# Gate projections moved from the projection stages into the attention tiles of a hybrid attention trunk

## The chip, the cores and the metric

The kernel runs on one core of a Trainium2 chip. The metric is the device time of one execution in microseconds (us), taken as the median of several. Engines are named as in the profile: PE (TensorE, matrix products and transposes), PEld (its weight loads), DVE (VectorE), ACT (ScalarE), POOL (GpSimd) and SP (SyncE, which issues the DMAs here). A change within 1% of the time before is about what a measurement of this kernel can't tell from no change.

## What is computed

The reference is a trunk of two residual layers over a sequence of 1024 frames with model width 1024, all in 32-bit floats. Cut to what matters:

```python
# layer 0
u = rms_norm(h, norm_g[0])
cq, ckv, kr, g_a, q_b, k_b, v_b, g_b = split_cols(u @ ab_w_in, AB_SIZES)
o_a = mla_attention(...)          # 8 heads, causal by chunks of 64
o_b = chunk_rel_attention(...)    # 8 heads, band of 9 chunks, relative bias
mixed = concat([o_a * silu(g_a), o_b * silu(g_b)]) @ ab_w_out
# layer 1
u = rms_norm(h, norm_g[1])
q, k, v, g, f = split_cols(u @ fox_w_in, FOX_SIZES)
o = forgetting_attention(...)     # 16 heads, causal, decay bias
mixed = (o * silu(g)) @ fox_w_out
# after each layer
h = h + mixed
h = h + (p[i] @ pe_w[i]) * sigmoid(rms_norm(h, pe_gate_norm[i]) @ pe_gate_w[i])
```

The gates `g_a`, `g_b` (512 columns each) and `g` (1024 columns) are projections of the same normed rows `u` as the queries, keys and values.

## The kernel before, in words

Every matrix product is made in three passes, so that its result is close to 32-bit: each operand is split into a high part (rounded to the matrix engine's `fp32r`) and a low part (what is left), and high x high, high x low and low x high are summed in PSUM. The split is always the same pair: ACT copies the value into `*_hi` (rounding), DVE subtracts that from the value into `*_lo`. `a_hi` and `a_lo` ([128, 8, 1024] each) hold a transposed 1024 x 1024 operand in SBUF for the whole kernel: first the normed rows `u`, later the gated attention outputs.

The program is a chain of stages with a barrier between them; inside a stage each engine runs its own written-out order, coupled by semaphores.

- `stage_ab` (tiles `pa_*`): the norm of `x`, the projections of layer 0 in chunks of weight columns (`Weights`: raw load by SP, `w_hi` by ACT at L173, `w_lo` by DVE at L179, two buffers), each chunk against all frames. Its last four chunks (`G0` and on) are the gates: 16 units of kind `"g"`, each 24 matmuls (L652) with 512 columns moving, then a Silu on ACT and a store to `s_g` in DRAM.
- `stage_attention("mla", ...)` and `stage_attention("chk", ...)`: the two attentions of layer 0, 8 heads each. `stage_attention("fox", ...)`: that of layer 1, 16 heads.
- `stage_oe("m", 0, ...)`: the output projection of layer 0 (units `"o"`), the embedding gate (`"e"`), then the projections of layer 1 (`"qk"`, `"v"` and 16 units `"g"`, L1589, stored to `f_g`). `stage_oe("t", 1, ...)`: output projection and embedding gate of layer 1.

The attention stages are what the change rewrites. A head has 8 tiles of 128 queries; tile `t` has `t + 1` blocks of 128 keys (at most 5 in `chk`). The tiles of all heads are numbered `s`, and every engine walks `s` up, in this order inside an iteration:

- PE: `score(s)` (L1009, with mask products at L1013) into one of two PSUM halves; `turn_p(s - 2)`, the transposes of the probabilities (L1024) in pieces of up to 4 blocks; in even iterations `spread_sums` (two transposes, L1032) and `times_v` (L1047) for the pair of tiles `s - 4`, `s - 3`.
- DVE: `row_max(s)` (L1130, in `chk` L1124); in odd iterations `invert` (L1135); `evacuate(s - 2)`, which makes `pt_lo` (L1144); in odd iterations `take_o` (L1152).
- ACT: in odd iterations `take_far` (L1090); `evacuate(s - 2)`, which makes `pt_hi` (L1080); `exp(s)` (L1069), which waits for `maxed` of tile `s`.

A score may only overwrite its half of PSUM when the exponentials of two tiles ago are done (`wait(pe, maxed if chk else exped, s - 1)`, that is tile `s - 2`). A piece is only turned when the piece two before it has been split (`pt_lo_done`). The PSUM tile `pv` has two buffers. Once per pair of heads, POOL forms gate x inverse sum (`gi`, L1184) and multiplies the output with it (L1188), ACT rounds it into `a_hi` (`give`, L1098) and POOL makes `a_lo` (L1190); for the last pair DVE does POOL's part (L1169 to L1175). SP loads `q`, `k`, `v` of a head and a gate row block of a pair, two buffers each, in the order of its loop over the heads.

Of the kernel before, what the change touches and what calls it, by code (L numbers as in the profile page):

```python
# [15 lines left out]
P = 128  # L16
D = 1024
# [38 lines left out]
def build(nc, x, p, positions, norm_g, ab_w_in, mla_q_norm, mla_w_uq, mla_kv_norm, mla_w_ukv,  # L56
# [12 lines left out]
    s_g = dram("s_g", [FH, 64, S])  # L69
# [5 lines left out]
    f_g = dram("f_g", [FH, 64, S])  # L75
# [31 lines left out]
    a_lo = G.sb("a_lo", [P, KD, S], F32R)  # L107
    ident = G.sb("ident", [P, P])
# [89 lines left out]
    def stage_ab():  # L198
        with ExitStack() as st:
# [10 lines left out]
            table += [cols(KD, w_in, at, 256) for at in (C_GB, C_GB + 256, C_GA, C_GA + 256)]  # L210
            LQ, LK, Q0, K0, MQ, V0, MK, V1, G0 = 0, 1, 2, 4, 6, 7, 8, 9, 10
# [3 lines left out]
            xr = sp.sb("xr", [P, 4, D])  # L215
            staged = xr
            sq = sp.sb("sq", [P, D])
            y = sp.sb("y", [P, 2, 768])
            l_hi = sp.sb("l_hi", [P, 5, S], F32R)
            l_lo = sp.sb("l_lo", [P, 5, S], F32R)  # L220
            g_norm = sp.sb("g_norm", [P, D])
# [4 lines left out]
            spare = sp.sb("spare", [P, 2 * CLIP + 8])  # L226
            t1 = spare[:, 0:512].rearrange("q (a n) -> q a n", a=2)
            rel = spare[0:HEADS, 0:2 * CLIP + 1]
# [36 lines left out]
            units += [("g", c, n) for c in range(G0, NCH) for n in range(4)]  # L265
# [20 lines left out]
            for u, (kind, c, n) in enumerate(units):  # L286
# [12 lines left out]
                if kind not in ("v", "g"):  # L299
                    due = u  # L300
# [4 lines left out]
                if kind == "lk" and n == ST - 1:  # L305
                    steps.append(("tables", 0))

# [4 lines left out]
            for what, n in steps:  # L312
                kind = units[n][0] if what in ("a", "b", "e", "t") else ""
                if what == "e" and kind not in ("v", "g"):
                    norm_at[n] = norms
                    norms += 1
                if what == "e" and kind in ("v", "g", "mk"):
                    outs_at["e", n] = outs
                    if kind != "g":
                        lo_at[outs] = len(lo_at)  # L320
                    stores.append(1)
                    outs += 1
# [42 lines left out]
            pair_g = s_g.rearrange("(c h) q n -> c (h q) n", h=2)  # L365

            with nc.Block() as block:

                @block.sync
                def _(sync):  # L370
# [37 lines left out]
                    sync.dma_start(rel, chk_rel_bias[0]).then_inc(rel_in, 16)  # L408

                    for what, n in steps:  # L410
                        if what == "xt" and n + 4 < ST:
                            sync.wait_ge(turned, jobs_at["xt", n] + 2)
                            load_x(n + 4)
                        if what == "w" and n + 1 < NCH:
# [7 lines left out]
                        if what == "e" and ("e", n) in outs_at:  # L422
# [10 lines left out]
                            else:  # L433
                                m = c - G0
                                pair = (4 + 2 * m if m < 2 else 2 * m - 4) + t // 2
                                store(o, pair_g[pair, :, (t % 2) * HALF:(t % 2 + 1) * HALF], src[:, 0:HALF])
# [19 lines left out]
                def _(act):  # L456
                    act.dma_start(g_norm[:], norm_g[0:1, :].to_broadcast([P, D])).then_inc(gain_in, 16)
# [6 lines left out]
                    def x_norm(t):  # L464
                        act.wait_ge(x_in[t % 4], 16 * (t // 4 + 1))
                        nc.scalar.activation(sq[:], xr[:, t % 4, :], ACT.Square, accum_out=x_ss[:, 0, t:t + 1])\
# [10 lines left out]
                    def evacuate(u):  # L477
# [3 lines left out]
                        if ("e", u) in outs_at:  # L481
                            o = outs_at["e", u]
                            slot_free(o)
                            if kind == "v":
# [3 lines left out]
                                return  # L488
                            if kind == "g":
                                nc.scalar.activation(staged[:, o % 4, 0:HALF], src[:, 0, :], ACT.Silu).then_inc(out_made, 1)  # L490
# [77 lines left out]
                def _(pe):  # L568
# [47 lines left out]
                    def unit(u, part):  # L616
# [28 lines left out]
                        elif kind == "v":  # L645
                            last = tokens(dst[:, 0:256], c, n, a_hi, a_lo, 0, 256)
                        else:
                            w_hi, w_lo = wt.halves(c)
                            block, cols = slice(n // 2 * P, (n // 2 + 1) * P), slice(n % 2 * HALF, (n % 2 + 1) * HALF)
                            for k in range(KD):  # L650
                                for w, a in ((w_hi, a_hi), (w_hi, a_lo), (w_lo, a_hi)):
                                    last = nc.tensor.matmul(dst, w[:, k, block], a[:, k, cols],  # L652
                                                            start=(k == 0 and w is w_hi and a is a_hi),
                                                            stop=(k == KD - 1 and w is w_lo))
# [14 lines left out]
                def _(dve):  # L669
# [8 lines left out]
                    def x_norm(t):  # L678
# [3 lines left out]
                        if t == 0:  # L682
# [3 lines left out]
                                                       in1=g_norm[:], op0=ALU.mult, op1=ALU.mult).then_inc(x_made, 1)  # L686
# [27 lines left out]
                    def evacuate(u):  # L714
                        kind, c, t = units[u]
                        if kind == "g":
                            return
# [156 lines left out]
    def stage_attention(kind, heads, first_pair, q_of, k_of, v_of, g_of, extra_of):  # L874

        mla, chk, fox = (kind == k for k in ("mla", "chk", "fox"))
        NT = ST
        NU = NT // 2
        NPAIR = heads // 2
        TILES = NT * heads  # L880

        def lowest(t):

            return max(0, t - BAND // P + 1) if chk else 0

        def turned(t):

            js = list(range(lowest(t), t + 1))
# [3 lines left out]
        BEFORE = [sum(len(turned(t)) for t in range(n)) for n in range(NT + 1)]  # L892

        def piece(s):

            return BEFORE[NT] * (s // NT) + BEFORE[s % NT]

        def in_units(rows):
            return rows.rearrange("q (u n) -> q u n", u=NU)

        with ExitStack() as st:
            sp = Space(st, kind)
            WIDE = BAND if chk else S
            KROWS = QK if mla else P
            XROWS = QK if mla else 67 if fox else 64
# [863 lines left out]
```

## Time and profile before

| what | us |
|---|---|
| median of 3 runs | 1992.22 |
| lowest and highest run | 1991.86, 2003.53 |
| the profiled execution, own time | 2002.86 |
| span of the profiled execution | 2001.1 |
| PE busy over the span | 1784.1 (89%) |
| DVE, ACT, POOL busy | 954.6, 834.7, 98.4 |
| mean granted clock of PE | 0.955 |

The span runs from the first to the last instruction of the program. A granted clock of 1.0 is 2.4 GHz, 0.5 is 1.2 GHz. In a line of the timeline the columns are start, duration, engine, line, operation, tiles (out<-in), shapes and count, and in brackets the idle time of the engine just before and what ended it. Consecutive instructions of one engine, line and tile are merged into a line.

### The profile page before, as it was taken

The page shows a single profiled execution, that of the slowest core. Times are in us where ns is not written, and L with a number is a line of the kernel's source. Part 1 is how long each engine was busy: PE and PEld are TensorE (multiplying, and loading weights), DVE is VectorE, ACT ScalarE, POOL GpSimd, SP SyncE. Part 2 cuts the span into 40 slices and gives each one's busy share as a digit, 9 for nine tenths or more (in the row PEclk, how much of TensorE's full clock was granted, in tenths as well). Part 3 has the DMA queues.
Part 4 walks back from the last instruction along what each step waited for, and adds up shares of the span by engine and source line. Part 5 has one row for each costly group of instructions (what it writes and reads, how often), then busy time and mean ns, then how long its engine had stood idle before and what let it go on. Part 6 is the DMA issues. An engine that isn't in the chain of part 4 may idle for free. (4 is left out here: it accounts for less than half of the span.)

```text
span 2001.1 us, 31843 instructions
## 1 busy us (share of the span) xinstructions
PE 1784.1 (89%) x12720; PEld 1639.9 (82%) x12720; DVE 954.6 (48%) x1797; ACT 834.7 (42%) x1702; POOL 98.4 (5%) x55
## 2 busy tenths in 40 slices
PE   5999778988996996999989999999968888869998
PEld 5999767867884775999989999998757777769898
DVE  5454556105774665234355444321057777722631
ACT  4433234216773765123153333312157778811410
POOL 0000000000210111000000000000002122100000
PEclk9999989998996998999999999999989999989999
DMA  5064368416423551510123443453174555251211
GB/s 179 22 200 144 116 161 216 126 59 163 122 79 100 149 131 37 185 53 27 48 106 106 127 126 120 125 141 100 47 175 121 140 138 128 64 179 48 64 64 38
DMA packets 178371, 223.94 MB, mean 112 GB/s; under 512 B 12856, under 2 KB 148296, under 8 KB 178224
## 3 DMA queue, kind: packets, MB, share of 16 engines
q1 hardware_dynamic: 177152, 218.43, 38.0%
q0 software_dynamic: 640, 2.62, 0.4%
q8 instruction: 102, 1.67, 0.4%
q10 hardware_dynamic: 432, 0.85, 0.1%
q14 instruction: 45, 0.37, 0.1%
HBM read 150.34 MB, written 77.29 MB: 114 GB/s over the span
## 5 line engine op out<-in xcount | busy, mean ns | idle before, releaser
L1556 PE MATMUL m_acc<-m_w_hi,g_a_hi 128*128 128x256 f32 (+1 forms) x1280 | 371.4, 290 | 19.1 <-DVE m_w_lo L179 14.6
L1556 PE MATMUL m_acc<-m_w_hi,g_a_lo 128*128 128x256 f32 (+1 forms) x1280 | 366.1, 286 | 0.0
L1556 PE MATMUL m_acc<-m_w_lo,g_a_hi 128*128 128x256 f32 (+1 forms) x1280 | 365.7, 286 | 0.0
L1556 PEld LDWEIGHTS m_acc<-m_w_hi,g_a_hi 128*128 128x128 f32 x1280 | 247.0, 193 | 19.5 <-DVE m_w_lo L179 14.8
L1556 PEld LDWEIGHTS m_acc<-m_w_lo,g_a_hi 128*128 128x128 f32 x1280 | 247.3, 193 | 0.0
L1556 PEld LDWEIGHTS m_acc<-m_w_hi,g_a_lo 128*128 128x128 f32 x1280 | 245.8, 192 | 0.0
L611 PE MATMUL pa_acc<-pa_w_hi,g_a_hi 128*128 128x256 f32 (+2 forms) x512 | 156.5, 306 | 15.9 <-DVE pa_w_lo L179 15.9
L1556 PE MATMUL t_acc<-t_w_hi,g_a_hi 128*128 128x256 f32 x512 | 147.2, 287 | 15.8 <-DVE t_w_lo L179 15.8
L611 PE MATMUL pa_acc<-pa_w_hi,g_a_lo 128*128 128x256 f32 (+2 forms) x512 | 151.8, 296 | 0.0
L611 PE MATMUL pa_acc<-pa_w_lo,g_a_hi 128*128 128x256 f32 (+2 forms) x512 | 151.5, 296 | 0.0
L1556 PE MATMUL t_acc<-t_w_hi,g_a_lo 128*128 128x256 f32 x512 | 145.8, 285 | 0.0
L1556 PE MATMUL t_acc<-t_w_lo,g_a_hi 128*128 128x256 f32 x512 | 145.1, 283 | 0.0
L1130 DVE TENSOR_REDUCE fox_neg_max<-fox_scores 128x1 f32<-128x128 f32 (+7 forms) x128 | 96.4, 753 | 54.0 <-PE fox_scores L1009 53.1
L1024 PE MATMUL fox_turn<-g_ident,fox_prob 128*128 128x128 f32 x576 | 89.3, 277 | 32.0 <-DVE fox_pt_lo L1144 31.9
L611 PEld LDWEIGHTS pa_acc<-pa_w_hi,g_a_hi 128*128 128x128 f32 x512 | 99.6, 195 | 16.4 <-issue 16.4
L1144 DVE TENSOR_TENSOR fox_pt_lo<-fox_turn,fox_pt_hi 128x128 fp32r<-128x128 f32 (+2 forms) x192 | 100.2, 550 | 25.2 <-ACT fox_pt_hi L1080 24.4
L1556 PEld LDWEIGHTS t_acc<-t_w_hi,g_a_hi 128*128 128x128 f32 x512 | 98.0, 191 | 16.0 <-DVE t_w_lo L179 16.0
L1069 ACT ACTIVATE fox_prob<-fox_scores,fox_neg_max 128x128 f32<-128x128 f32 (+7 forms) x128 | 94.9, 741 | 35.6 <-DVE fox_neg_max L1130 32.7
L1024 PEld LDWEIGHTS fox_turn<-g_ident,fox_prob 128*128 128x128 f32 x576 | 66.5, 141 | 43.7 <-issue 31.0
L611 PEld LDWEIGHTS pa_acc<-pa_w_lo,g_a_hi 128*128 128x128 f32 x512 | 100.0, 195 | 0.0
L611 PEld LDWEIGHTS pa_acc<-pa_w_hi,g_a_lo 128*128 128x128 f32 x512 | 98.9, 193 | 0.0
L1556 PEld LDWEIGHTS t_acc<-t_w_lo,g_a_hi 128*128 128x128 f32 x512 | 98.7, 193 | 0.0
(284 smaller groups left out, 4154.3 us busy)
## 6 DMA issues: line engine op xcount, KB each, us to landing
m_w_raw<-in_fox_w_in SPq DMA_DIRECT2D x16, 1024.0 KB, 6.0
pa_w_raw<-in_ab_w_in SPq DMA_DIRECT2D x10, 1024.0 KB, 5.7
f_v<-m_pr SPq DMA_DIRECT2D x32, 256.0 KB, 3.1
fox_q<-f_q SPq DMA_DIRECT2D x32, 256.0 KB
fox_k<-f_k SPq DMA_DIRECT2D x32, 256.0 KB
fox_v<-f_v SPq DMA_DIRECT2D x16, 512.0 KB, 3.3
s_mq<-pa_xr SPq DMA_DIRECT2D x32, 192.0 KB, 3.0
s_mk<-pa_xr SPq DMA_DIRECT2D x32, 192.0 KB, 3.0
```

The costliest lines, as they stand in the source:

```text
L611: last = nc.tensor.matmul(dst, a[:, k, t * P:(t + 1) * P], w[:, k, n0:n0 + n], start=(k == 0 and a is m_hi and w is w_hi), stop=(k == kt - ...
L1024: last = nc.tensor.transpose(turn[:, g % 2, m, :], prob[:, s % 3, (j - lo) * P:(j - lo + 1) * P], ident[:])
L1069: nc.scalar.activation(prob[:, s % 3, 0:n], src, ACT.Exp, bias=neg_max[:, s % 4:s % 4 + 1], scale=-1.0 if chk else 1.0, accum_out=total[:, ...
L1130: nc.vector.tensor_reduce(r, scores[:, t % 2, 0:n], AX_X, ALU.max, negate=True).then_inc(maxed, 1)
L1144: nc.vector.tensor_tensor(pt_lo[where], turn[:, g % 2, 0:len(js), :], pt_hi[where].bitcast(F32), ALU.subtract).then_inc(pt_lo_done, 1)
L1556: last = nc.tensor.matmul(dst, a[:, k, t * P:(t + 1) * P], w[:, k0 + k, 0:n], start=(k == 0 and a is m_hi and w is w_hi), stop=(k == kt - ...
```

## The change

1. The gate chunks leave `stage_ab` and `stage_oe` (units `"g"`, `s_g`, `f_g` and their stores and loads are gone).
2. The attention of a layer computes its gates itself. Per head SP loads 256 KB of gate weights (`load_gate`: half of the rows of a block of 128 columns, in pieces of 512 bytes), ACT and DVE split them (`gate_hi`, `gate_lo`), and PE runs one step of 3 matmuls of 512 columns in each tile (`gate_part`), 8 tiles for one unit of 128 x 512 gates, in one PSUM bank `gacc`. In the iteration after the one with the eighth step ACT takes tanh(g/2) (`gate_tanh`) and DVE forms (tanh + 1) x g (`gate_times`); the factor 0.5 that makes this a SiLU is put into `take_far`'s scale.
3. `mla` and `chk` become one stage of 16 heads, `ab`.
4. Outputs gather in a new SBUF tile `og`, shared by all stages: `take_o` adds into it, POOL divides each pair of tiles (`divide`) and applies each finished gate unit (`apply_gate`). The split into `a_hi` and `a_lo` moves to the start of `stage_oe`, 8 steps `"os"`, of which two come before its first unit. Scratch tiles of the other stages now lie in `og`, and the loads of `pr` and of the norm gains wait for the last of these splits. `rel` is loaded after the last x tile.
5. To fit, `pv` has one buffer, `prob` two instead of three, so `row_max` in `chk` now waits for the turning of tile `s - 2`; `far` keeps two units.

The diff, cut to its core:

```diff
+        LATE = 2
+        def gate_unit(s):
+            f = s - LATE
+            return divmod(f, KD) if 0 <= f < KD * NH else None
+        def split_gate(s):
+            c, at = divmod(s, 2 * NT)
+            n = 2 * c + 2 + (at == 11)
+            return n if at in (4, 11) and n < NH else None
...
-            pv = sp.ps("pv", [P, 2, 2, 2 * P])
+            pv = sp.ps("pv", [P, 2, 2 * P])
+            gacc = sp.ps("gacc", [P, HALF])
...
+                    def load_gate(n):
+                        wait(sync, w_lo_done, n)
+                        rows = gates[n // 2].rearrange("(k q) n -> q k n", q=P)[:, 4 * (n % 2):4 * (n % 2) + 4, :]
+                        sync.dma_start(w_raw[:], rows).then_inc(in_w, 16)
...
-                    for hd in range(heads):
+                    for hd in range(NH):
                         load_qk(hd)
-                        if chk:
+                        if kinds[hd] == "chk":
                             load_extra(hd)
+                        if hd == 0:
+                            load_gate(0)
                         load_v(hd)
-                        if hd % 2 == 0:
-                            load_gate(hd // 2)
+                        if hd == 0:
+                            load_gate(1)
+                        elif hd < NH - 1:
+                            load_gate(hd + 1)
...
+                    def gate_part(s):
+                        unit, kt = gate_unit(s)
+                        c, half = divmod(unit, 2)
+                        if kt == 0:
+                            pe.wait_ge(w_lo_done, 2 * c + 2)
+                            wait(pe, g_made, unit)
+                        cols = slice(half * HALF, (half + 1) * HALF)
+                        for w, a in ((w_hi, a_hi), (w_hi, a_lo), (w_lo, a_hi)):
+                            last = nc.tensor.matmul(gacc[:], w[:, c % 2, kt, :], a[:, kt, cols],
...
+                        if kt == KD - 1:
+                            last.then_inc(g_summed, 1)
...
                     def spread_sums(uu):
-                        wait(pe, o_done, uu - 1)
+                        wait(pe, o_done, uu)
...
                         if 0 <= s - 2 < TILES:
                             turn_p(s - 2)
+                        if gate_unit(s) is not None:
+                            gate_part(s)
                         if s >= 4 and s % 2 == 0:
                             spread_sums((s - 4) // 2)
                             times_v((s - 4) // 2)
...
+                    def gate_tanh(unit):
+                        act.wait_ge(g_summed, unit + 1)
+                        wait(act, gated, unit - 2)
+                        nc.scalar.activation(gate[:, unit % 3, :], gacc[:], ACT.Tanh, scale=0.5).then_inc(g_tanh, 1)
...
                         if s < TILES:
                             exp(s)
...
+                        if s < 2:
+                            gate_hi(s)
+                        if split_gate(s) is not None:
+                            gate_hi(split_gate(s))
+                        if s >= KD + LATE and (s - LATE) % KD == 0:
+                            gate_tanh((s - LATE) // KD - 1)
...
+                    def gate_times(unit):
+                        dve.wait_ge(g_tanh, unit + 1)
+                        nc.vector.scalar_tensor_tensor(out=gate[:, unit % 3, :], in0=gate[:, unit % 3, :], scalar=1.0,
+                                                       in1=gacc[:], op0=ALU.add, op1=ALU.mult).then_inc(g_made, 1)
...
                         if s >= 5 and s % 2 == 1:
                             take_o((s - 5) // 2)
...
+                        if s >= KD + LATE and (s - LATE) % KD == 0:
+                            gate_times((s - LATE) // KD - 1)
...
+                    def divide(uu):
+                        at = og[r, hd // 2, cols]
+                        nc.gpsimd.tensor_tensor(at, at, far[r, uu % 2, 1, :], ALU.mult).then_inc(divided, 1)
+                    def apply_gate(unit):
+                        at = og[:, m, half * HALF:(half + 1) * HALF]
+                        nc.gpsimd.tensor_tensor(at, at, gate[:, unit % 3, :], ALU.mult).then_inc(gated, 1)
...
-            steps = [("w", 0)]
+            steps = [("w", 0), ("os", 0), ("os", 1)]
...
                 steps.append(("a", u))
+                if c == O0 and n < ST // 2 - 1:
+                    steps += [("os", 2 * n + 2), ("os", 2 * n + 3)]
...
+                            if c == O0:
+                                pe.wait_ge(o_lo, 2 * n + part + 1)
```

## Rows read from the trace of the kernel before

**Rows 1.** Windows, three attentions: PE, PEld, DVE, ACT, POOL busy, clock, DMA share, GB/s.
```profile
446.20:603.10 156.90, 138.34 (x973) 119.54 (x974) 103.75 (x212) 111.91 (x250) 21.54 (x9) 0.95 0.44 122
...
629.00:795.00 166.00, 148.80 (x877) 119.14 (x877) 102.95 (x291) 106.54 (x260) 21.39 (x9) 0.89 0.42 105
...
1452.60:1766.00 313.40, 257.15 (x1856) 218.84 (x1856) 223.60 (x452) 231.64 (x521) 49.97 (x21) 0.96 0.51 125
```

**Rows 2.** Tile m_acc, the gate products of the second layer.
```profile
L1589 PE MATMUL m_acc<-g_a_hi,m_w_hi x128: 389/397/400, 1358.3 to 1447.6; 128*128 128x512 f32 x128
...
L1589 PE MATMUL m_acc<-g_a_hi,m_w_lo x128: 392/397/400, 1358.8 to 1448.0; 128*128 128x512 f32 x128
```

**Rows 3.** Timeline, end of the projections to the start of attention.
```profile
343.37 0.28 PE L611 MATMUL pa_acc<-pa_w_hi,g_a_lo 128*128 128x256 f32 x1
...
446.22 0.34 SPq L949 DMA_DIRECT2D mla_q<-s_mq  x1
...
455.47 0.47 PE L1009 MATMUL mla_scores<-mla_k,mla_q 96*128 96x128 f32 x1 [13.01 <-DMA mla_kx<-s_mk]
```

**Rows 4.** Timeline of DVE: first to second attention, and the end.
```profile
603.14 1.23 DVE L1130 TENSOR_REDUCE mla_neg_max<-mla_scores 128x1 f32<-128x1024 f32 x1 [0.76 <-PE mla_scores L1009]
...
628.97 0.29 DVE L1124 CUSTOM_DVE_ANT_0 chk_prob<-chk_scores,chk_extra 128x128 f32<-128x128 f32 x1 [10.64 <-PE chk_scores L1009]
...
788.87 0.43 DVE L1152 TENSOR_TENSOR chk_o<-chk_pv,chk_far 64x256 f32<-64x256 f32 x1 [1.87 <-ACT chk_far L1090]
...
793.00 1.23 DVE L1175 TENSOR_TENSOR g_a_lo<-chk_o,g_a_hi 128x1024 fp32r<-128x1024 f32 x1 [1.12 <-ACT g_a_hi L1098]
```

**Rows 5.** Timeline of the first attention, third tile of a head.
```profile
551.11 1.04 PE L1024 MATMUL mla_turn<-g_ident,mla_prob 128*128 128x128 f32 x8
...
552.37 1.29 DVE L1144 TENSOR_TENSOR mla_pt_lo<-mla_turn,mla_pt_hi 128x512 fp32r<-128x512 f32 x2 [0.57 <-ACT mla_pt_hi L1080]
...
553.21 0.30 PE L1024 MATMUL mla_turn<-g_ident,mla_prob 128*128 128x128 f32 x1 [0.42 <-DVE mla_pt_lo L1144]
...
553.35 0.39 PE L1032 MATMUL mla_pv<-g_ident,mla_inverse 128*128 128x128 f32 x2
...
553.91 0.54 DVE L1130 TENSOR_REDUCE mla_neg_max<-mla_scores 128x1 f32<-128x384 f32 x1
...
554.49 0.58 ACT L1069 ACTIVATE mla_prob<-mla_scores,mla_neg_max 128x384 f32<-128x384 f32 x1
```

**Rows 6.** The same place in the second layer.
```profile
1536.59 0.39 PE L1032 MATMUL fox_pv<-g_ident,fox_inverse 128*128 128x128 f32 x2
...
1537.99 0.58 ACT L1069 ACTIVATE fox_prob<-fox_scores,fox_neg_max 128x384 f32<-128x384 f32 x1 [0.92 <-DVE fox_neg_max L1130]
```

**Rows 7.** Timeline of PE: its waits near the end of a head.
```profile
567.14 0.63 PE L1024 MATMUL mla_turn<-g_ident,mla_prob 128*128 128x128 f32 x4 [0.92 <-DVE mla_pt_lo L1144]
...
1549.67 0.52 PE L1024 MATMUL fox_turn<-g_ident,fox_prob 128*128 128x128 f32 x3 [1.02 <-DVE fox_pt_lo L1144]
```

**Rows 8.** Lines 1643 and 1458: 128x512 from PSUM on DVE and ACT, ns.
```profile
L1643 DVE SCALAR_TENSOR_TENSOR m_p_hi<-m_tp,g_gcol,m_pr x32: 745/750/753, 1059.9 to 1260.8; 128x512 fp32r<-128x512 f32 x32
...
L1458 ACT ACTIVATE m_pr<-m_acc x16: 597/597/598, 1364.1 to 1448.5; 128x512 f32<-128x512 f32 x16
L1458 ACT ACT_TABLE_LOAD  x1: 1283/1283/1283, 1358.9 to 1358.9; - x1
```

**Rows 9.** Windows of tile chk_pv: one group at either clock.
```profile
706.59:709.27 2.68, 2.68 (x14) 2.68 (x14) 0.00 (x0) 0.00 (x0) 0.53 1.03 219
711.90:713.44 1.54, 1.54 (x14) 1.54 (x14) 0.43 (x1) 0.00 (x0) 1.00 0.30 98
```

**Rows 10.** Windows of PE: after idle stretches of 3 us.
```profile
113.00:116.40 3.40, 3.39 (x29) 1.00 0.54 214
...
1051.20:1054.60 3.40, 3.36 (x16) 0.50 0.00 0
```

**Rows 11.** DMA issues in the first attention, us to landing.
```profile
mla_v<-s_v SPq DMA_DIRECT2D x8, 512.0 KB, 3.7
```

More of the change, by code:

```diff
@@ L298, in stage_ab @@
                 steps.append(("e", u))
[L299 removed]
+                if kind not in ("v",):
                     due = u
@@ L644, in unit @@
                                 last = tokens(acc[:, banks[u][i], :], c, n, l_hi[:, 3:5], l_lo[:, 3:5], HALF * i, HALF)
-                        elif kind == "v":
+                        else:
                             last = tokens(dst[:, 0:256], c, n, a_hi, a_lo, 0, 256)
[L647 to L654, printed above, removed]
                         last.then_inc(summed, 1)
@@ L871, in stage_ab, with stage_attention, chk, lowest @@
             sp.end()
-    def stage_attention(kind, heads, first_pair, q_of, k_of, v_of, g_of, extra_of):
-        mla, chk, fox = (kind == k for k in ("mla", "chk", "fox"))
+    def stage_attention(tag, heads, gates):
         NT = ST
         NU = NT // 2
[L879 to L888, printed above, removed]
+        NH = len(heads)
+        TILES = NT * NH
+        LATE = 2
+        kinds = [head[0] for head in heads]
+        def chk(s):
+            return kinds[s // NT] == "chk"
+        def lowest(s):
+            return max(0, s % NT - BAND // P + 1) if chk(s) else 0
+        def turned(s):
+            js = list(range(lowest(s), s % NT + 1))
             cut = (len(js) + 1) // 2 if len(js) > 4 else 4
             return [js[n:n + cut] for n in range(0, len(js), cut)]
[L892 to L899, printed above, removed]
+        PIECE = [0]
+        for s in range(TILES):
+            PIECE.append(PIECE[-1] + len(turned(s)))
+        QKDMA = {"mla": 4, "chk": 5, "fox": 7}
+        def qk_loaded(hd):
+            return 16 * sum(QKDMA[kind] for kind in kinds[hd % 2:hd + 1:2])
+        def x_loaded(hd):
+            return 16 * sum(kind == "chk" for kind in kinds[hd % 2:hd + 1:2])
+        def gate_unit(s):
[5 more added lines that the diff above has]
+            return n if at in (4, 11) and n < NH else None
         with ExitStack() as st:
[L902 to L905, printed above, removed]
+            sp = Space(st, tag)
             q = sp.sb("q", [P, 2, S], F32R)
@@ new lines, in apply_gate @@
+                    def apply_gate(unit):
+                        m, half = divmod(unit, 2)
+                        pool.wait_ge(divided, NU * (2 * m + 1) + 2 * half + 2)
+                        pool.wait_ge(g_made, unit + 1)
+                        at = og[:, m, half * HALF:(half + 1) * HALF]
+                        nc.gpsimd.tensor_tensor(at, at, gate[:, unit % 3, :], ALU.mult).then_inc(gated, 1)
+                    for uu in range(NU * NH):
+                        divide(uu)
+                        if uu % (2 * NU) in (NU + 1, 2 * NU - 1):
+                            apply_gate(uu // (2 * NU) * 2 + (uu % (2 * NU) == 2 * NU - 1))
@@ L1581, in unit @@
                                 return
[L1582 removed]
+                        else:
                             last = tokens(dst[:, 0:table[c][1]], c, n, a_hi, a_lo, 0, KD, table[c][1])
[L1584 to L1591 removed]
                         last.then_inc(summed, 1)
```

336 lines of the change are left out of this document (149 added, 187 removed).

## The prediction

> **What bounds the kernel now.** I read the page for the stages, then windows over the attentions, then the timeline of one head on all engines, because the change moves work between stages with different limits. In the three attention stages PE is busy for 138 of 157, 149 of 166 and 257 of 313 us, starts and ends included, against 104, 103 and 224 for DVE [rows 1]. So PE has no large idle time there to give away: the reader should see that the attention tiles are already nearly full of matrix work, cut up by short waits. The granted clock is lowest, 0.89, in the second attention, though no PE idle stretch inside its heads reaches 1 us.
>
> The gate products are pure PE work as well. In the second layer 384 matmuls of 512 columns start between 1358.3 and 1448.0 us, 89.7 / 383 = 0.234 us each [rows 2]. The question is therefore not what they cost but what idle time they fill, and what new waits they bring.
>
> **What goes.** The gate units of the projections. First layer: the last other matmul starts at 343.4 and the attention's first load at 446.2 [rows 3]. What remains is the drain of the last k/v tile (its scaling, transposes and four stores, about 9 us by the same drain elsewhere in the stage, instead of the 3.7 us after the last gate): 93 us gone. Second layer: 90 us. The join of the two attentions: row_max of the last mla tile starts at 603.1, that of the first chk tile at 629.0, 25.8 us; in a running stage the next tile would come 2.7 us later, so 23 go, and with chk's slow first head (21.5 against 18.2 us, from the starts of its row_max) 26. The ends: from the last take_o, 788.9, to the end of a_lo, 794.2 [rows 4], 5.4 us become about 2.3 of POOL (multiplications of 256 and 512 columns; those of 1024 take 2.4), 3 us in each layer, 6 in all. Together 93 + 90 + 26 + 6 = 215 us.
>
> **What comes: the products.** Each of 256 tiles gets 3 matmuls, 3 x 0.234 = 0.70 us, so 179 us. That is nearly the 183 removed.
>
> **What comes: a wait at each unit.** There is one PSUM bank for the gates. In iteration s = 8k + 2 (the third tile of a head) PE must begin the next unit, and `g_made` lets it only when tanh and `gate_times` of the old unit are done. Both stand in their queues behind work that hangs on this same iteration's score: tanh behind `exp(s)`, that behind `row_max(s)`. Walk it in the first attention [rows 5], where the eight transposes of tile 7 are followed by the next score at 551.90. With the new step of tile 9 in between, score(10) ends at 551.90 + 0.70 + 0.72 = 553.3, the one transpose by 553.45. DVE is held by pt_lo of tile 7 (to 553.66) and `take_o`, so row_max(10) stays at 553.91 to 554.45 and the exponential at 554.49, with the read of its sum to 555.15. Then tanh, 0.60, and `gate_times`, 0.75 [rows 8], with 0.1 for the hand-over: PE goes on at 556.65. It idles for 3.2 us, and the times_v that began at 553.35 begins at 557.35, 4.0 us later, two gate steps included. Behind PE's wait stand times_v and the next score, and everything else waits for those; ACT and DVE are not full (71% and 66% in [rows 1]), but they have nothing to do then. In the second layer the exponential starts at 1537.99 and times_v at 1536.59 [rows 6]: 1537.99 + 0.67 + 0.60 + 0.10 + 0.75 + 0.05 + 0.70 = 1540.86, 4.3 us later, of which 3.6 are idle. chk by the same steps gives 4.05.
>
> The other six steps of a head cost 6 x 0.70 = 4.2, less what they hide. Near the head's end PE waits 0.92 us for pt_lo in mla and 1.02 in fox [rows 7]; a step in front hides 0.70 of it; fox has 0.5 more in smaller waits. Per head: mla 4.0 + 4.2 - 0.7 = 7.5, chk 4.05 + 4.2 - 0.55 = 7.7, fox 4.3 + 4.2 - 1.2 = 7.3. A stage has 15 such waits; first heads have none. Sum: 7 x 7.5 + 8 x 7.7 + 15 x 7.3 = 224 us.
>
> First heads: 4.2 - 1 for the steps, and a wait of their own. SP loads the second weight half only when DVE has split the first, after the first tile; ACT stands in front of exp(2) until it lands. Load 3.7 to 4.4, two splits of 0.6 and 0.7, against a PE that would be there after 2.5: 5 us. With the steps 8 per stage, 16 us.
>
> **Weight halves later on.** The odd halves are issued right behind the v load of a new head, which waits for times_v of the stalled iteration, and ACT asks for them one iteration later. The v load lands after 3.7 us [rows 11]; a half behind it, smaller but in short pieces, perhaps after 4. ACT is held for 1.5 to 2.3 us in front of exp of the fifth tile. PE needs that exponential 1 to 2 iterations later, so between 0 and 2.1 us show, 0.7 taken, 14 times: 10 us (0 to 30).
>
> **The rest.** `os`: one ACT copy and one DVE subtraction in front of the first output unit, of which 1.6 us show, twice: 3 us; the later ones lie beside units of 5.7 us on PE. `divide` and `apply_gate` lie on POOL, which is idle for over 90% of the time; take_o of the same pair is ready 2 us before the single `pv` is wanted again. The third prob buffer: row_max in chk waits for one to five more transposes, which end before DVE is free in the stalled tile and otherwise are needed only 4 us later: 0, at most 0.5 per tile (32 us).
>
> **The clock.** A times_v group of 14 took 2.68 us at a granted clock of 0.53 and 1.54 at 1.00 [rows 9]: a fall costs 1.1. After two idle stretches of PE of 3.0 us the clock was 1.00 in one case and 0.50 in the other [rows 10]. The new waits are as long, so half of 30 are taken to bring a fall: 15 x 1.1 = 17 us; the bounds are 0 and 34. The Trainium skill, "TensorE: Matmul & The Clock Gate" (What's actually happening), says that the slow clock is the default and only activity lifts it. Taken strictly it speaks against this change, since it would let every one of these idle waits end at the slow clock; the sum would be 17 us more.
>
> **Sum.** 224 + 16 + 10 + 3 + 17 = 270, less 215: +55 us. On the profiled execution's 2002.9 that is 2058; that execution lies 10.6 us above the median of the runs, so the forecast is 2047.
>
> **Rivals.**
> A. The wait for `g_made` doesn't show (faster). With more work on PE, ACT and DVE may run ahead, so that the unit is ready when PE arrives. For: both have a third of their time free. Against: exp(s) can't run ahead of score(s), which PE does just before. Price: the idle 7 x 3.2 + 8 x 3.3 + 15 x 3.6 = 103 and the 17 of the clock go: 1927. It decides once the waits average less than 3.4 x (1 - 55 / 120) = 1.8 us.
> B. Part of it: hand-overs and waits overlap more than I walked, and about half of the wait shows: 2047 - 60 = 1987.
> C. Every wait brings the clock down: 2064. The rule above is this case.
> D. The weight halves land late, and 3 us show each time: 14 x 2.3 = 32 more, 2079.
> E. Tanh and exp don't share ACT's function table. A table load takes 1.28 us in this trace; two more in each of 30 waits is 77, so 2124. The Trainium skill, "ScalarE: Activation LUTs" (Table sets: the hidden batching unit), lists tanh in the set of exp, and by it no load comes.
> F. The change does not move the work (the steps stay at the stage's end): excluded by the order in the diff.
>
> **Chances.** Forecast 0.50, A 0.13, B 0.11, C 0.14, D 0.09, E 0.03. More than 1% faster is below 1972, more than 1% slower above 2012, the least that a measurement of this kernel can tell from no change: faster 0.14, same 0.11, slower 0.75. The range leaves out A and E: 1985 to 2090.
>
> **What would show it.** In the profile after: no gate products before 450 us; PE idle stretches of about 3 us before the gate matmuls in the third tile of every head, ended by DVE's `gate_times`, 15 in each attention stage; heads of about 26 us in the first layer and 25 in the second instead of 19 and 18; ACT waiting for `w_raw` in the fourth tile of even heads; one table load per attention stage. It would be wrong if the gate matmuls started without a wait in the third tile, if heads were shorter than 24 us, or if the attentions together grew by less than 215 us.

## The result, and the profile after

The changed kernel takes 2103.09 us, median of 4 runs (2101.98 to 2105.20); the kernel before takes 1995.45 us (1991.86 to 2003.53, 4 runs). The ratio is 1.0526, with a 95% interval of 1.0502 to 1.0550. It is slower, as forecast, but by 107.6 us in place of 55, and the time lies outside the range of 1985 to 2090. The profiled execution took 2101.98 us, with a span of 2100.1 us against 2001.1 before.

To see which term is off, cut both traces at the first and the last row maximum of each attention. The timeline of VectorE in the kernel before, for the cuts that [rows 4] doesn't have:

```profile
778.89 0.82 DVE L1124 CUSTOM_DVE_ANT_0 chk_prob<-chk_scores,chk_extra 128x640 f32<-128x640 f32 x1 [0.92 <-PE chk_scores L1009]
...
1463.45 0.29 DVE L1130 TENSOR_REDUCE fox_neg_max<-fox_scores 128x1 f32<-128x128 f32 x1 [8.57 <-PE fox_scores L1009]
...
1745.39 1.23 DVE L1130 TENSOR_REDUCE fox_neg_max<-fox_scores 128x1 f32<-128x1024 f32 x1 [0.25 <-PE fox_scores L1009]
```

and the same places in the changed kernel:

```profile
363.65 0.29 DVE L1158 TENSOR_REDUCE ab_neg_max<-ab_scores 128x1 f32<-128x128 f32 x1 [14.77 <-PE ab_scores L1016]
...
820.79 0.82 DVE L1154 CUSTOM_DVE_ANT_0 ab_prob<-ab_scores,ab_extra 128x640 f32<-128x640 f32 x1 [2.18 <-PE ab_turn L1030]
...
1415.60 0.29 DVE L1158 TENSOR_REDUCE fox_neg_max<-fox_scores 128x1 f32<-128x128 f32 x1 [8.46 <-PE fox_scores L1016]
...
1844.13 1.23 DVE L1158 TENSOR_REDUCE fox_neg_max<-fox_scores 128x1 f32<-128x1024 f32 x1 [1.29 <-PE fox_scores L1016]
```

The first row maximum comes 92.8 us earlier (363.7; 456.5 before, read like [rows 4]). The first layer's attentions take 457.1 us in place of 322.4. The stretch between the layers takes 594.8 in place of 684.6, the second attention 428.5 in place of 281.9, and the rest is 0.3 us longer. What went is as forecast, to within a microsecond or two. What came is the whole miss, and it lies inside the heads. Windows over the two attentions of the changed kernel, and over two neighbouring heads of the first (columns as in [rows 1]):

```profile
363.70:829.50 465.80, 407.02 (x2284) 326.44 (x2283) 225.12 (x543) 236.97 (x543) 65.13 (x78) 0.90 0.31 78
641.00:673.00 32.00, 28.34 (x135) 21.86 (x135) 13.24 (x38) 14.49 (x36) 5.59 (x7) 0.79 0.33 78
673.00:699.40 26.40, 22.88 (x135) 17.59 (x135) 13.25 (x39) 14.45 (x36) 2.79 (x5) 1.00 0.38 92
1415.60:1854.00 438.40, 368.29 (x2233) 308.19 (x2233) 237.75 (x479) 243.03 (x543) 65.32 (x78) 0.91 0.34 82
```

The two heads have the same 135 matmul groups. They lie in the part with `chk` heads. One took 26.4 us at a granted clock of 1.00, which is what the prediction walked out for such a head (19 + 7.7). The other took 32.0 us at 0.79. The clock was forecast to fall in half of the waits.

The waits themselves are on the page, in the costliest groups of instructions. The last column is TensorE's idle time before the gate products:

```profile
L1042 PE MATMUL ab_gacc<-g_a_hi,ab_w_hi 128*128 128x512 f32 x128 | 66.8, 522 | 48.7 <-DVE ab_gate L1192 44.7
L1042 PE MATMUL fox_gacc<-g_a_hi,fox_w_hi 128*128 128x512 f32 x128 | 63.7, 498 | 51.3 <-DVE fox_gate L1192 46.8
```

`gate_times` ended 15 of them in each stage, for 44.7 and 46.8 us. One wait in the timeline, the answer to [rows 6]:

```profile
1500.59 0.58 ACT L1090 ACTIVATE fox_prob<-fox_scores,fox_neg_max 128x384 f32<-128x384 f32 x1 [0.66 <-DVE fox_neg_max L1158]
1501.07 0.19 ACT L1090 ACTIVATION_READ_ACCUMULATOR fox_prob<-fox_scores,fox_neg_max 128x1 f32 x1
1501.16 0.59 ACT L1117 ACTIVATE fox_gate<-fox_gacc 128x512 f32<-128x512 f32 x1
1501.78 0.69 DVE L1192 SCALAR_TENSOR_TENSOR fox_gate<-fox_gate,fox_gacc 128x512 f32<-128x512 f32 x1 [1.03 <-ACT fox_gate L1117]
...
1502.62 0.76 PE L1042 MATMUL fox_gacc<-g_a_hi,fox_w_hi 128*128 128x512 f32 x1 [3.00 <-DVE fox_gate L1192]
```

It is the chain of the forecast, link by link: exponential, its sum, tanh, multiplication, TensorE. But the product that follows takes 0.76 us instead of 0.47. Windows of TensorE from there on, over the next products and `times_v` (PE busy, clock, DMA share, GB/s):

```profile
1502.60:1506.00 3.40, 3.38 (x13) 0.50 0.02 5
1506.00:1509.40 3.40, 3.40 (x18) 0.66 0.10 20
648.90:662.50 13.60, 13.60 (x46) 0.52 0.20 60
```

The third row follows a wait of 3.0 us in the first attention: the engine was busy for all of 13.6 us, at half speed for nearly all of it. In the trace's records of the granted clock 26 low stretches begin inside the heads, 12 in the first layer and 14 in the second, of 3.4 to 13.7 us and 150.2 us in all; TensorE was busy for 141.5 us of them. 24 began during one of the 30 waits for `gate_times` or within 1.5 us of its end. The other two, both in the second layer, began 2.0 us after a shorter wait, for ScalarE's exponential. One of these, with the window behind it:

```profile
1567.84 0.50 PE L1016 MATMUL fox_scores<-fox_k,fox_q 128*128 128x512 f32 x1 [1.36 <-ACT fox_prob L1090]
...
1569.80:1573.20 3.40, 3.40 (x13) 0.50 0.02 5
```

The kernel before has 3 low stretches of 3.4 us there, all in its second attention, where no single wait of TensorE inside the heads reached 0.9 us.

### The profile page after: what moved, and what is told of

Same layout as the page of the kernel before. It is cut to its first block and busy times, and to the rows that moved or that the text cites. A ratio compares the mean times of both kernels' runs of the same rounds, so it can differ in the third digit from the quotient of the medians.

```text
span 2100.1 us, 32171 instructions
## 1 busy us (share of the span) xinstructions
PE 1826.9 (87%) x12720; PEld 1665.2 (79%) x12720; DVE 979.9 (47%) x1860; ACT 841.1 (40%) x1724; POOL 139.9 (7%) x176
## 5 line engine op out<-in xcount | busy, mean ns | idle before, releaser
L1101 ACT ACTIVATE ab_pt_hi<-ab_turn 128x384 fp32r<-128x384 f32 (+2 forms) x192 | 82.5, 463 | 77.8 <-PE ab_turn L1030 76.8
L1172 DVE TENSOR_TENSOR fox_pt_lo<-fox_turn,fox_pt_hi 128x128 fp32r<-128x128 f32 (+2 forms) x192 | 99.9, 548 | 22.8 <-ACT fox_pt_hi L1101 21.7
L1222 POOL TENSOR_TENSOR g_og<-g_og,fox_far 64x256 f32<-64x256 f32 x64 | 46.7, 730 | 956.4 <-DVE g_og L1180 956.4
L1597 PEld LDWEIGHTS t_acc<-t_w_hi,g_a_hi 128*128 128x128 f32 x512 | 98.5, 192 | 13.7 <-issue 13.7
L1042 PE MATMUL ab_gacc<-g_a_hi,ab_w_hi 128*128 128x512 f32 x128 | 66.8, 522 | 48.7 <-DVE ab_gate L1192 44.7
L1042 PE MATMUL fox_gacc<-g_a_hi,fox_w_hi 128*128 128x512 f32 x128 | 63.7, 498 | 51.3 <-DVE fox_gate L1192 46.8
L1101 ACT ACTIVATE fox_pt_hi<-fox_turn 128x128 fp32r<-128x128 f32 (+2 forms) x192 | 87.9, 489 | 35.7 <-PE fox_turn L1030 33.8
```

What stands on the lines that cost most here:

```text
L1042: last = nc.tensor.matmul(gacc[:], w[:, c % 2, kt, :], a[:, kt, cols], start=(kt == 0 and w is w_hi and a is a_hi), stop=(kt == KD - 1 and ...
L1101: nc.scalar.activation(pt_hi[u % 2][:, at:at + len(js), (s % 2) * P:(s % 2 + 1) * P], turn[:, g % 2, 0:len(js), :], ACT.Copy).then_inc(pt_ ...
L1172: nc.vector.tensor_tensor(pt_lo[u % 2][where], turn[:, g % 2, 0:len(js), :], pt_hi[u % 2][where].bitcast(F32), ALU.subtract).then_inc(pt_l ...
L1222: nc.gpsimd.tensor_tensor(at, at, far[r, uu % 2, 1, :], ALU.mult).then_inc(divided, 1)
L1597: last = nc.tensor.matmul(dst, a[:, k, t * P:(t + 1) * P], w[:, k0 + k, 0:n], start=(k == 0 and a is m_hi and w is w_hi), stop=(k == kt - ...
```

## The experiments

Ten kernels were run, each beside runs of the kernel before on the same chip (medians 1996.03 and, for the last two, 1999.09 us).

**1. The clock's share.** TensorE is kept busy during the wait with work that nobody reads; the wait stays.

```
                             pe.wait_ge(w_lo_done, 2 * c + 2)
+                            if unit and s - 2 < TILES:
+                                pe.wait_ge(pt_lo_done, PIECE[s - 2])
+                                for r in range(23):
+                                    nc.tensor.transpose(turn[:, (PIECE[s - 2] + 1) % 2, r % 4, :], ident[:], ident[:])
                             wait(pe, g_made, unit)
```

Expected:

> Edit: while PE would wait for the unit it makes 23 transposes that nobody reads (into the free half of the transpose PSUM), after the previous half has been split; order, waits and all other work stay. Theory 1 (24 of 30 waits bring the granted clock down to 0.5 for 3.4 us, and the dense work after the wait pays 1.5 us for each): the clock stays at 1.00 in the attention heads, 25 to 40 us faster than the changed kernel, 2063 to 2078. Theory 2 (a fall costs little, because what follows is limited by ACT and DVE anyway): within 8 us of 2103, or slower by the transposes that overrun the wait.

Measured: 2041.36 us, ratio 1.0219 (1.0182 to 1.0256), 62 us less than the changed kernel. Windows from the first to the last row maximum of each attention:

```profile
363.40:783.70 420.30, 405.06 (x2585) 330.01 (x2585) 220.34 (x530) 232.75 (x534) 62.53 (x75) 0.99 0.34 87
1377.40:1782.80 405.40, 376.57 (x2522) 316.85 (x2522) 231.62 (x467) 237.83 (x533) 62.63 (x75) 0.98 0.37 89
```

Two low stretches are left in the heads, both begun within 2.2 us of the end of a wait of 1.3 to 1.4 us for the exponential, and the attentions take 420.3 and 405.4 us in place of 457.1 and 428.5: 60 us, for 24 fewer stretches, or 2.5 us each. Nothing but TensorE's idle time was changed, so this 60 is the clock. Theory 1 had the mechanism and, with 25 to 40 us, too small a size. The 60 fits the low stretches themselves: TensorE did 141.5 us of work in them at half speed, so at most half of that, 71 us (an estimate), could be lost.

The same with 10 transposes, so that part of each wait stays idle:

> As the run that kept TensorE busy with 23 unread transposes during each wait (2041 us), but with only 10, so that something near 2 us of each wait stays idle; nothing waits longer for it. Theory 1 (the cost of the clock falls with the idle time that is left in a wait, and is nearly gone at 2 us): 2041 to 2055 us. Theory 2 (any idle stretch at this place brings the fall with it): 2080 to 2105 us. In the trace: 2 to 6 falls in the heads by theory 1, over 20 by theory 2.

Measured: 2048.96 us, ratio 1.0269 (1.0248 to 1.0289). The page has no large wait here, so this is the answer for the tile:

```profile
  DVE fox_gate L1196: 21.7, 15
```

TensorE still idled 21.7 us in 15 waits (1.4 us each; 22.2 us in the first layer), and the clock fell 5 times in the heads, 3 times after one of these waits and twice after one for the exponential. This is theory 1 in time and in falls, though less idle time was left than the 2 us that it speaks of. At this size of wait most of the loss is gone already.

**2. The order.** First the odd half of the next weights, on which ScalarE had stood for 0.6 to 2.1 us in each odd head after the first (all its waits for gate weights, those of the first heads included, were 23 with 30.0 us in the changed kernel):

```
-            n = 2 * c + 2 + (at == 11)
-            return n if at in (4, 11) and n < NH else None
+            n = 2 * c + 2 + (at == 13)
+            return n if at in (4, 13) and n < NH else None
```

> Edit: the odd half of the gate weights is split in the sixth tile of its head (s % 16 = 13) instead of the fourth (11); nothing else. Theory 1 (the late weight half costs far more than the 0.7 us per head that I took, about 3, because ACT and DVE both stand still in front of the exponential and row_max that PE needs next): 14 odd heads get 2.5 to 3.5 us shorter, the kernel 35 to 50 us faster than the changed kernel, near 2060, and odd heads of the second layer fall from 29.0 to about 26. Theory 2 (odd heads are longer for another reason, such as the two-tile rhythm of the buffers, or the price only moves to the sixth tile): within 10 us of 2103.

Measured: 2088.40 us, ratio 1.0454 (1.0391 to 1.0517). That is 15 us less than the changed kernel by the medians, between the two theories, but with two runs that lie 9 us apart and an interval that overlaps that of the changed kernel (from 1.0502). ScalarE's waits for gate weights fell from 30.0 to 6.7 us, and the waits for `gate_times` stayed (44.8 and 46.8 us). The clock still fell 28 times in the heads, and was low for 174 us there in place of 150, so the 15 us are net of more low clock. The stall is a side matter.

Then the first step of a unit behind `times_v` in TensorE's order, so that independent work stands ahead of the wait:

```
-                        if gate_unit(s) is not None:
+                        first = gate_unit(s) is not None and gate_unit(s)[1] == 0
+                        if gate_unit(s) is not None and not first:
                             gate_part(s)
...
                             times_v((s - 4) // 2)
+                        if first:
+                            gate_part(s)
```

> Edit: only the first gate step of each unit goes behind times_v in PE's order; tanh and gate_times stay where they are. Theory 1 (PE idles 3.1 to 3.5 us per unit because it asks for the unit before ACT and DVE can have finished it): times_v of 2.3 us fills the wait, so 0.8 to 1.2 us of idle is left, 30 x 2.3 = 69 us less, and the falls of the clock go as well, up to 37 more: 2000 to 2035. Theory 2 (the wait is only moved: ACT and DVE need PE's next score, which now comes no earlier): 2085 to 2105.

Measured: 1969.57 us, ratio 0.9859 (0.9826 to 0.9892): 133.5 us less than the changed kernel. The tile's answer in the second layer:

```profile
  DVE fox_w_lo L1190: 4.6, 1
  DVE fox_gate L1195: 3.8, 15
```

46.8 us of waits became 3.8 (44.7 became 7.8 in the first layer), 80 us less in all, and no low stretch begins any more between the first and the last row maximum of either attention. The time lies below theory 1's 2000 to 2035: the waits shrank by more than it expected, and it priced the clock at 37 at most. 80 and the clock's 62 would be 142; the other 8 were not traced.

The other end of the same wait, with TensorE's order as in the changed kernel: tanh and its multiplication come first in their iteration.

```
                     for s in range(TILES + 4):
+                        if s >= KD + LATE and (s - LATE) % KD == 0:
+                            gate_tanh((s - LATE) // KD - 1)
...
-                        if s >= KD + LATE and (s - LATE) % KD == 0:
-                            gate_tanh((s - LATE) // KD - 1)
```

and the same for `gate_times` on VectorE.

> The order of TensorE stays as in the changed kernel; only the tanh of a finished unit and its multiplication come first in their iteration of ScalarE and VectorE, ahead of the row sum, the row maximum and the halves that stand ahead of them now. Theory 1 (time goes where TensorE waits, and each wait costs itself and a fall of the clock): the 30 waits shrink from 3.1 to 3.5 us to about 2.3, which gives 30 x 0.9 = 27 us, and of the 62 us of the clock a part in proportion or more, together 45 to 75 us: 2030 to 2060 us. Theory 2 (the clock answers to any recurring wait of this size, whether 3.3 or 2.3 us long): only the waits shrink, 2070 to 2085 us. Theory 3 (the wait is not what costs; ScalarE and VectorE hold the heads): no gain, 2100 us.

Measured: 1992.69 us (8 runs), ratio 0.9980 (0.9963 to 0.9997): 110 us less, beyond all three. The timeline and the tile's answer show why:

```profile
1498.92 0.42 PE L1016 MATMUL fox_scores<-fox_kx,fox_qx 67*128 67x384 f32 x1
...
1499.18 0.61 ACT L1117 ACTIVATE fox_gate<-fox_gacc 128x512 f32<-128x512 f32 x1
...
1500.17 0.69 DVE L1192 SCALAR_TENSOR_TENSOR fox_gate<-fox_gate,fox_gacc 128x512 f32<-128x512 f32 x1
...
1500.97 0.19 PEld L1042 LDWEIGHTS fox_gacc<-g_a_hi,fox_w_hi 128*128 128x128 f32 x1 [1.64 <-issue]
1501.00 0.47 PE L1042 MATMUL fox_gacc<-g_a_hi,fox_w_hi 128*128 128x512 f32 x1 [1.48 <-DVE fox_gate L1192]
```

```profile
  DVE fox_gate L1192: 20.0, 15
  DVE fox_w_lo L1187: 4.4, 1
```

Tanh no longer stands behind an exponential that hangs on this iteration's row maximum. The waits shrank to 20.0 and 17.6 us (from 46.8 and 44.7), which is 54 us, not the 27 expected; one low stretch is left in the heads, and that one followed a wait of 1.3 us for the exponential. 54 and the clock's 60 are the 110 within 4 us. Theory 1 had the mechanism and half of the size.

Both orders together, the second step on the way to the best version:

> Edit: as before, and tanh goes in front of ACT's copies and exponential of that iteration, gate_times in front of DVE's row_max. Theory 1: PE arrives after gate_times has ended, no PE wait over 1 us is left at a unit's start, a further 20 to 30 us less than with the PE order alone: 1975 to 2010. Theory 2 (what is taken from PE's wait comes back, since row_max of the third tile now starts 0.75 us later and everything hangs on it): no faster than with the PE order alone.

Measured: 1949.51 us, ratio 0.9759 (0.9719 to 0.9799). No gate product of a later unit waits any more. That is 20 us less than with TensorE's order alone, as theory 1 had it; its range of 1975 to 2010 started from a time too high for that order. Against the run that keeps TensorE busy and keeps the waits it is 92 us less, and the waits of the changed kernel were 91.5 us.

**3. What the products cost.** On that version's order, 23 of each unit's 24 products are left out:

```
-                        for w, a in ((w_hi, a_hi), (w_hi, a_lo), (w_lo, a_hi)):
-                            last = nc.tensor.matmul(gacc[:], w[:, c % 2, kt, :], a[:, kt, cols],
-                                                    start=(kt == 0 and w is w_hi and a is a_hi),
-                                                    stop=(kt == KD - 1 and w is w_lo))
                         if kt == KD - 1:
-                            last.then_inc(g_summed, 1)
+                            nc.tensor.matmul(gacc[:], w_hi[:, c % 2, kt, :], a_hi[:, kt, cols],
+                                             start=True, stop=True).then_inc(g_summed, 1)
```

> Leaves out 23 of the 24 gate products of each of the 32 units (so the gates are wrong); loads, halves, tanh and multiplication stay. On the order of the run with both changes of order, 1949.5 us. Theory 1 (after the waits are gone TensorE bounds the heads, so each product costs its full 0.234 us): 32 x 23 x 0.234 = 172 us less, 1778 us, with heads of 18.1 to 19.3 us as before the change. Theory 2 (ScalarE and VectorE bound the heads by then, with the halves, the tanh and the multiplications that came to them, 2.6 us of ScalarE and 2.1 us of VectorE per head): heads of about 21 us, 32 x 3 = 96 us less, 1850 us.

Measured: 1931.08 us, ratio 0.9678 (0.9659 to 0.9697). 172 us of matmuls went, and 18 us of time. Neither theory had that. The timeline of that kernel, where the odd half of the weights is split:

```profile
534.16 0.63 ACT L1123 ACTIVATE ab_w_hi<-ab_w_raw 128x512 fp32r<-128x512 f32 x1 [1.80 <-DMA ab_w_raw<-in_ab_w_in]
...
534.83 0.69 DVE L1187 TENSOR_TENSOR ab_w_lo<-ab_w_raw,ab_w_hi 128x512 fp32r<-128x512 f32 x1 [2.56 <-ACT ab_w_hi L1123]
535.43 0.82 DVE L1158 TENSOR_REDUCE ab_neg_max<-ab_scores 128x1 f32<-128x640 f32 x1
...
536.28 0.79 ACT L1090 ACTIVATE ab_prob<-ab_scores,ab_neg_max 128x640 f32<-128x640 f32 x1 [1.11 <-DVE ab_neg_max L1158]
...
537.22 0.79 PE L1016 MATMUL ab_scores<-ab_k,ab_q 96*128 96x512 f32 x1 [2.40 <-ACT ab_prob L1090]
```

ScalarE stands for the transfer, VectorE stands for ScalarE with the row maximum behind it, and 2.40 us of TensorE go idle where the products had been. The clock falls with it (0.89 and 0.91 over the two attentions, as in the changed kernel): 16 low stretches begin in the heads, 119.5 us in all, with TensorE busy for 110 us of them, so up to 55 us (an estimate) are the clock. With the products in place this wait was mostly hidden under them. So it was repeated with the split at position 13:

> The run with one gate product of 24 once more (the gates are wrong again), now with the odd half of the weights split at position 13, when it has landed. In the run before, ScalarE stood 1.8 us for that half, TensorE then idled 2.6 us behind it and the clock fell in nearly every second head. Theory 1 (that wait is what kept the 172 us of products from showing): heads near the 18 to 19 us of the kernel before in place of 20 to 24.5, about 30 x 3.5 = 105 us less than the 1931 us, 1800 to 1850 us. Theory 2 (ScalarE and VectorE hold the heads by their own work): 1900 to 1930 us.

Measured: 1866.55 us, ratio 0.9339 (0.9310 to 0.9368), 80 us less than the next kernel, which differs from it only in having all products. That is 0.11 us for each of 736 products that last 0.234. The clock takes a part of the gain: without the products 7 low stretches begin in the heads, with TensorE busy for 22 us of them, and none with the products, so up to 11 us (an estimate) belong to it. Even so about half of the products' time doesn't show. That it lies beside waits which TensorE has in any case is the reading here; no run separates the products by their place. The time lies between the theories: the heads are at 20.7 and 20.2 us, above the 18 to 19 of the kernel before.

**4. The best version.** Both orders, and the odd half at position 13:

> The run with both changes of order, with the odd half of the next unit's weights split at the iteration after next (position 13 of 16 instead of 11), when its transfer has landed. Theory 1 (ScalarE's wait of 1.3 to 2.1 us for the transfer still delays the heads): 30 x 0.5 to 1.0 = 15 to 30 us less, 1920 to 1935 us. Theory 2 (with TensorE as the bound, a wait of ScalarE is inside its slack): 1945 to 1955 us, no change that can be measured.

Measured: 1946.88 us, ratio 0.9750 (0.9733 to 0.9766): within theory 2, and by the time nothing that can be told from the version without it. The traces say more. From the first to the last row maximum the two attentions take 728.7 us in place of 738.7, mostly because the odd heads of the second layer fell from 23.5 to 22.2 us; in this execution the first row maximum came 4.9 us later (367.2 in place of 362.3), before any code in which the two versions differ, and that hid half of it. Then with the first unit's weights ahead of everything:

```
+                    load_gate(0)
                     for hd in range(NH):
                         load_qk(hd)
...
+                    gate_hi(0)
+                    gate_hi(1)
                     for s in range(TILES + 4):
```

and `gate_lo(0)`, `gate_lo(1)` ahead of VectorE's loop.

> The best run so far (both changes of order, odd half split at position 13, 1947 us) with the first unit's two weight halves loaded ahead of the first head's queries and keys, and split before the first row maximum, while the stage waits for its first transfer. Theory 1 (the waits of 4.3 and 4.7 us for them are on the path that sets the end): 9 us less, 1936 to 1940 us. Theory 2 (the transfers of queries and keys start later by as much): no change, 1944 to 1950 us.

Measured: 1942.03 us, ratio 0.9712 (0.9690 to 0.9733), 5 us less by the medians, and 8 by the ratios, since the two versions ran on different chips. The first heads went from 24.5 to 19.2 and from 23.6 to 18.8 us, but the first score now waits longer for its keys:

```profile
365.94 0.48 PE L1015 MATMUL ab_scores<-ab_k,ab_q 96*128 96x128 f32 x1 [17.29 <-DMA ab_kx<-s_mk]
```

That is 2 us more than the 15.21 us of the run before it. The 10 us of the heads are theory 1, and the later transfers of theory 2 take 2 of them back. This version is 2.9% faster than the kernel before, and 7.7% faster than the change as it was made, with the same products.

## Why the prediction was right in sign and wrong in size

By its own steps, in us against the kernel before. Column A is the sum of the prediction without its 17 for the clock; B is the changed kernel; C is the run that keeps TensorE busy.

| stretch | A, forecast | B, changed | C, kept busy |
|---|---|---|---|
| until the first row maximum | -93 | -92.8 | -93.1 |
| first to last row maximum, layer 1 | +101 | +134.7 | +97.9 |
| from there to the second layer's first | -91.5 | -89.8 | -90.9 |
| first to last row maximum, layer 2 | +122.5 | +146.6 | +123.5 |
| rest | -1.5 | +0.3 | -0.1 |
| sum | +38 | +99.0 | +37.3 |

A for layer 1 is 7 x 7.5 + 8 x 7.7 + 8 for the first head, less 26 for the join, and 5 for the halves. For layer 2 it is 15 x 7.3 + 8 + 5. The middle is -90 - 3 + 1.5.

- **What goes** (215): right.
- **The products and the wait at each unit** (224): right in the first layer, some 12 us too high in the second. The 30 waits were forecast at 3.2 to 3.6 us of idle and came at 3.0 (44.7 / 15) and 3.1 (46.8 / 15) on average. With the clock out of the way the mean head is 26.6 us in the first layer (19 and 19, plus 7.5 and 7.7) and 25.7 in the second (18 + 7.3). The products were taken at their full 0.70 us per step less 0.55 to 1.2 per head. In the order of the changed kernel the sum over a head bears that out in the first layer; in the better order about half of their time is hidden, which the prediction had not asked about.
- **First heads** (16): right. They grew by 8.0 and 8.9 us, forecast 8 each; the waits for the second half were 4.0 and 4.5 us, forecast 5.
- **Weight halves later on** (10): too low, and balanced by luck, so the mean heads above hide two errors. In the run that keeps TensorE busy most odd heads of the second layer take 26.6 us and the even ones 24.4, against 18.1 and 17.9 before: an odd head pays 2.0 us for its half, forecast 0.7, and an even one grew by 6.5, forecast 7.3. The first four odd heads of the first layer pay 0.6 each, the rest about nothing. The halves come to some 16 us (an estimate), 6 more than forecast, while products and wait in 15 heads of the second layer come to 12 less. Rival D, at 32 more in all, is out: the two stretches C of the attentions sum to 221 us, forecast 224.
- **The third `prob` buffer** (0): no loss can be seen. In the kept-busy run the inner `chk` heads take 26.2 to 26.4 us, forecast 26.7 without it. VectorE does wait there for the turning (114.9 us over 54 waits in the changed kernel); a version with three buffers was not run.
- **Tables**: ScalarE loads a table twice in the two attention stages, at the exponential and never at tanh (before, twice in three stages); rival E is out.
- **The clock** (17, bounds 0 and 34): this is the step that failed. The prediction priced a fall at 1.1 us, as a single `times_v` group at low clock, and let half of the 30 waits bring one. Measured: 26 low stretches in place of 15, 24 of them at the 30 waits, and 2.5 us for each, 60 to 62 in all. Even its upper bound, one fall at 1.1 for each wait, was little more than half of that. The price was wrong because a low stretch doesn't end with the group: 150.2 us over 26 stretches is 5.8 us each, and TensorE was busy for 141.5 us of it. The clock's own bounds were taken from one group [rows 9] and from two earlier idle stretches [rows 10], and neither row shows how long the low clock lasts.

In the profiled executions the miss is 2102 - 2058 = 44 us, which is 62 - 17 = 45. Against the median the miss is 56 us. The other 12 come from the correction: the prediction took 10.6 us off because the profiled execution of the kernel before was a long one, but that of the changed kernel lies 1.1 us below its median.

Rival C (every wait brings the clock down, 2064) was nearer in the count, 30 for 24, and had the same wrong price. Rivals A and B fell with the 30 waits. The point from which A was said to decide, waits below 1.8 us, has a near test: with tanh first they averaged 1.25 us, and the kernel came out level with the one before.

As for the rule of the Trainium skill that the prediction weighed ("TensorE: Matmul & The Clock Gate", What's actually happening: the slow clock is the default, and only activity lifts it): the runs bear out that activity decides. Work that nobody reads, put into the waits, kept the clock at 0.98 to 0.99 and gave 62 us. Taken as strictly as the prediction took it, that every idle wait ends at the slow clock, it goes too far: 6 of the 30 waits of 2.8 to 3.3 us brought no fall, and neither did 27 of the 30 of 1.3 to 1.6 us.

## What to carry to other kernels

Independent work that is put between the steps of a tuned loop may fit in its throughput and still lose by one wait in its order. Before the change is judged, ask what the engine's next instruction is when the buffer isn't free, and put the waiting step behind work that can go on. Two reorderings, of three loops, turned 5.3% slower into 2.4% faster. Price a recurring idle stretch of TensorE of some 3 us at itself and something for the clock, here two thirds as much again (92 us of waits, 60 of clock), and take the length of a low stretch from rows, not the length of the group that happens to show it.

## What had not been expected of the hardware

Of 30 waits of 2.8 to 3.3 us, 24 brought a low stretch of the clock. Of 30 waits of 1.3 to 1.6 us, which followed ten transposes, 3 did, and of 30 waits of 0.9 to 1.5 us none. But waits of 1.2 to 2.0 us for the exponential, in another tile of the second layer, brought one now and then in the same three kernels (2, 2 and 1 times) and in the kept-busy run (2 times), so the length of one wait alone doesn't decide. In the first attention stage the low stretches from 648 us on, all in `chk` heads, were the longest, 10.2 and 13.7 us, while TensorE was busy for all of 13.6 us in the window shown above; why they lasted longer there than after equal waits elsewhere, where most were 3.4 us, wasn't tried and stays open. Matmuls can also be about half free: 172 us of them cost 80 us in an order without waits, and 18 us where they covered another wait and kept the clock up.
